# RWKV-7 scan on one core: the next level's products moved ahead of a step's outputs, state and scores on TensorE, and ScalarE reading the score banks before VectorE

## The reference, cut to what matters

```
def step(S, inp):
    r_t, w_t, k_t, v_t, kk_t, a_t = inp
    sa = einsum('bhvk,bhk->bhv', S, -kk_t)
    S = S * w_t[:, :, None, :] + sa[..., None] * (kk_t * a_t)[:, :, None, :] + v_t[..., None] * k_t[:, :, None, :]
    return S, einsum('bhvk,bhk->bhv', S, r_t)
S, y = lax.scan(step, S0, (tm(r), tm(decay), tm(k), tm(v), tm(kk), tm(a)))
```

## Time and profile before

| | us |
|---|---|
| median of 3 runs (lowest to highest) | 3029.55 (3027.71 to 3032.02) |
| the profiled execution | 3030.38 |
| its span on the core | 3028.3 |
| from the first level 0 addition of step 0 to that of step 15 (line 2957) | 918.78 to 1117.71 |

### The profile page before, as it was taken

How to read it: one execution, slowest core, us unless ns; L and a number is a source line. 1 busy time by engine, 2 the same in 40 slices (tenths; PEclk the granted TensorE clock), 3 DMA queues, 4 the chain that set the end, 5 groups by cost and what they waited for, 6 DMA issues and landing times.

```text
span 3028.3 us, 72949 instructions
## 1 busy us (share of the span) xinstructions
PE 2878.5 (95%) x29617; PEld 2731.4 (90%) x29617; DVE 1534.1 (51%) x2080; ACT 1083.7 (36%) x2139; POOL 1323.2 (44%) x959
## 2 busy tenths in 40 slices
PE   6998999998988988999999999989999999899998
PEld 6998999997978876799998899889999899799998
DVE  3435666127357775666603252476651444566612
ACT  4224333225455552433323443243332422433322
POOL 3443444442435563344443263434444344344443
PEclk8999999999999999999999999999999999899999
DMA  7544333543411004333344313433234543233332
GB/s 268 165 153 161 93 91 91 163 127 126 125 38 28 4 14 131 120 91 91 103 153 152 110 56 116 165 125 92 88 117 142 170 123 90 63 92 91 91 90 85
DMA packets 465618, 332.56 MB, mean 110 GB/s; under 512 B 19914, under 2 KB 435608, under 8 KB 465122
## 3 DMA queue, kind: packets, MB, share of 16 engines
q1 hardware_dynamic: 461400, 325.24, 34.8%
q10 hardware_dynamic: 4010, 4.22, 0.6%
HBM read 319.62 MB, written 10.20 MB: 109 GB/s over the span
## 4 chain that ended last, share of the span: by engine, by line
PE 57%; issue 4%; DVE 3%; POOL 3%; ACT 2%; DMA 0%; POOLq 0%; ACTq 0%; DVEq 0%
PE banks L1666 33%; PE banks L1674 17%; POOL ct L894 2%; PE banks L1627 1%; DVE h L2658 1%; PE banks L1689 1%; PE banks L1972 1%; DVE proj L2602 1%; PE banks L2125 0%; POOL mmt L885 0%; PE banks L1760 0%; DMA s_state<-in_state_wkv_b_dram 0%; PE banks L1695 0%; DVE proj_b L2602 0%; PE banks L2327 0%
## 5 line engine op out<-in xcount | busy, mean ns | idle before, releaser
L765 POOL TENSOR_TENSOR w_lo<-w_raw,w_hi 128x1024 fp32r<-128x1024 f32 x395 | 1005.9, 2547 | 1106.3 <-ACT w_hi L981 1086.0
L1666 PE MATMUL banks<-u_hi,w_hi 128*128 128x260 f32 x4064 | 832.7, 286 | 14.8 <-ACT w_hi L981 9.8
L1666 PE MATMUL banks<-u_lo,w_hi 128*128 128x260 f32 x4064 | 823.7, 284 | 0.0
L1666 PEld LDWEIGHTS banks<-u_hi,w_hi 128*128 128x128 f32 x4064 | 625.7, 189 | 27.6 <-issue 15.2
L1666 PEld LDWEIGHTS banks<-u_lo,w_hi 128*128 128x128 f32 x4064 | 628.4, 189 | 1.5
L981 ACT ACTIVATE w_hi<-w_raw 128x1024 fp32r<-128x1024 f32 x402 | 424.5, 1056 | 456.0 <-PE banks L1674 292.2
L1674 PE MATMUL banks<-u_hi,w_lo 128*128 128x260 f32 x4064 | 528.0, 282 | 0.0
L1674 PEld LDWEIGHTS banks<-u_hi,w_lo 128*128 128x128 f32 x4064 | 502.4, 187 | 1.6
L1666 PE MATMUL banks<-hid_hi,w_hi 128*128 128x260 f32 x1664 | 336.3, 283 | 0.0
L1666 PE MATMUL banks<-hid_lo,w_hi 128*128 128x260 f32 x1664 | 335.2, 283 | 0.0
L3107 DVE TENSOR_TENSOR csb<-proj 128x520 f32 (+1 forms) x42 | 30.6, 728 | 470.6 <-ACT proj L1048 470.6
(11 more groups left out here) (463 smaller groups left out, 3914.7 us busy)
## 6 DMA issues: line engine op xcount, KB each, us to landing
w_raw<-in_ffn_w_up_dram SPq DMA_DIRECT2D x176, 512.0 KB, 3.7
ada_raw<-in_ada_w_dram SPq DMA_DIRECT2D x96, 512.0 KB, 4.8
w_raw<-in_ffn_w_down_dram SPq DMA_DIRECT2D x64, 448.0 KB, 3.7
w_raw<-in_sconv_w_in_dram SPq DMA_DIRECT2D x48, 512.0 KB, 5.3
ada_ahead<-in_ada_w_dram SPq DMA_DIRECT2D x36, 512.0 KB, 7.3
ada_ahead_down<-in_ada_w_dram SPq DMA_DIRECT2D x36, 512.0 KB, 6.3
w_raw<-in_ffn_w_down_dram SPq DMA_DIRECT2D x32, 512.0 KB, 4.1
ada_pro<-in_ada_w_dram SPq DMA_DIRECT2D x6, 2048.0 KB, 21.5
```

What stands on the lines that cost most here:

```text
L765: pool.tensor_tensor(w_lo[:, s, :, :], w_raw[:, s, :, :], w_hi[:, s, :, :].bitcast(F32), ALU.subtract).then_inc(lo_done, 1)
L1666: pe.matmul(tile_ps[slot][half][0:width, 0:HALF], w_hi[:, s, k, 0:width], x[:, k0 + k, half * HALF:(half + 1) * HALF], start=start and k = ...
```

## The change

On TensorE a step's order becomes: update products of level 0; first products of level 1; outputs of step w - 1; first half of score part 0; update products of level 1; state products; second half of part 0; first products of level 2; right side parts 0 and 1; first half of part 1; update products of level 2; right side parts 2 and 3; second half of part 1; first products of level 3; first half of part 2; update products of level 3; second half of part 2; all of part 3; block solutions and past; values turned; passed on; inverse turned; first products of level 0 of w + 1; solutions. The values are turned in bank 7 and the inverse in bank 4, the reverse of before. ScalarE copies a score part as soon as it is made, and VectorE masks it after that. ScalarE copies the outputs of step w - 1 in step w, after its level 1 copy, and takes score part 3 before the block solution. VectorE updates the state after level 1's additions in place of level 0's, and masks a part one level later (part 3 after `receptances`). Step 0 and the last three steps are unrolled on ScalarE. The sample operations keep their places. The core of the diff:

```diff
     j, hh = n // 2, n % 2
     pair, b, rs = slice(2 * j, 2 * j + 2), bank[4 + (n + 1) % 4], slice((1 - hh) * HD, (2 - hh) * HD)
-    act.wait_ge(scores_masked, 4 * w + n + 1)
+    act.wait_ge(sc_done, 4 * w + n + 1)
...
-        ins = act.activation(uv[q][rs, :, hh, :], bank[4][rs, 0:4 * HD].rearrange("p (i t) -> p i t", i=4),
+        ins = act.activation(uv[q][rs, :, hh, :], bank[7][rs, 0:4 * HD].rearrange("p (i t) -> p i t", i=4),
...
-    act.activation(mmt[q][:, :, HD:2 * HD], bank[7][:, 4 * HD:8 * HD].rearrange("p (i t) -> p i t", i=4),
+    act.activation(mmt[q][:, :, HD:2 * HD], bank[4][:, 4 * HD:8 * HD].rearrange("p (i t) -> p i t", i=4),
...
-def scan_step(c, q, one_more, two_more):
+def outputs_out(w, c, q):
+    act.wait_ge(y_mm, 2 * w + 2)
+    act.activation(rw_y[:, 4 * q:4 * q + 4, ds(HD * c, HD)],
+                   bank[6][:, 0:4 * HD].rearrange("p (i t) -> p i t", i=4), ACT.Copy)\
+       .then_inc(y_ready, 1)
+def scan_step(c, q, one_more=True, two_more=True, first=False):
     w = 2 * c + q
     for lvl in range(1, NLV):
         first_products_out(w, lvl)
+        if lvl == 1 and not first:
+            outputs_out(w - 1, c + q - 1, 1 - q)
...
+    if one_more:
+        scores_out(w + 1, 1 - q, 3)
     block_solution_out(w)
     if one_more:
-        scores_out(w + 1, 1 - q, 3)
     solution_out(w, q)
-    act.wait_ge(y_mm, 2 * w + 2)
-    act.activation(rw_y[:, 4 * q:4 * q + 4, ds(HD * c, HD)],
-                   bank[6][:, 0:4 * HD].rearrange("p (i t) -> p i t", i=4), ACT.Copy)\
-       .then_inc(y_ready, 1)
-
...
-with act.Fori(0, NCH - 1) as c:
-    for q in range(2):
-        scan_step(c, q, True, True)
-for q in range(2):
-    scan_step(NCH - 1, q, q == 0, False)
+scan_step(0, 0, first=True)
+with act.Fori(0, NCH - 2) as c:
+    scan_step(c, 1)
+    scan_step(c + 1, 0)
+scan_step(NCH - 2, 1)
+scan_step(NCH - 1, 0, two_more=False)
+scan_step(NCH - 1, 1, one_more=False, two_more=False)
+outputs_out(2 * NCH - 1, NCH - 1, 1)
...
-        mm = both(lambda rs: bank[7][far(rs), (4 + i) * HD:(5 + i) * HD], lambda rs: mmt[q][rs, i, 0:HD],
+        mm = both(lambda rs: bank[4][far(rs), (4 + i) * HD:(5 + i) * HD], lambda rs: mmt[q][rs, i, 0:HD],
...
-        mm = both(lambda rs: bank[4][rs, i * HD:(i + 1) * HD],
+        mm = both(lambda rs: bank[7][rs, i * HD:(i + 1) * HD],
...
     update_products(w, q, 0)
+    first_products(w, q, 1)
     if w:
         outputs_of_solution(w - 1, qn)
+    if one_more:
+        scores_among(w + 1, qn, 0)
+    update_products(w, q, 1)
+    if w:
         state_products(qn)
     if one_more:
-        scores_among(w + 1, qn, 0)
         scores_of_keys(w + 1, qn, 0)
-    for lvl in range(1, NLV):
-        first_products(w, q, lvl)
-        if lvl == 1:
-            pe.wait_ge(st_updated, w + 1)
-            right_side(q, (0, 1))
-        if one_more:
-            if lvl == 1:
-                pe.wait_ge(y_ready, w + 1)
-                pe.wait_ge(srow_copied, 1)
-            elif lvl == 2:
-                pe.wait_ge(st_updated, w + 2)
-            else:
-                pe.wait_ge(rhs_ready, 2 * w + 1)
-            scores_among(w + 1, qn, lvl)
-        update_products(w, q, lvl)
-        if one_more:
-            scores_of_keys(w + 1, qn, lvl)
-        if lvl == 1:
-            right_side(q, (2, 3)).then_inc(rhs_mm, 1)
+    first_products(w, q, 2)
+    pe.wait_ge(st_updated, w + 1)
+    right_side(q, (0, 1))
+    if one_more:
+        pe.wait_ge(y_ready, w + 1)
+        pe.wait_ge(srow_copied, 1)
+        scores_among(w + 1, qn, 1)
+    update_products(w, q, 2)
+    right_side(q, (2, 3)).then_inc(rhs_mm, 1)
+    if one_more:
+        scores_of_keys(w + 1, qn, 1)
+    first_products(w, q, 3)
+    if one_more:
+        pe.wait_ge(st_updated, w + 2)
+        scores_among(w + 1, qn, 2)
+    update_products(w, q, 3)
+    if one_more:
+        scores_of_keys(w + 1, qn, 2)
+        pe.wait_ge(rhs_ready, 2 * w + 1)
+        scores_among(w + 1, qn, 3)
+        scores_of_keys(w + 1, qn, 3)
     if one_more:
         pe.wait_ge(scores_masked, 4 * w + 6)
         pe.wait_ge(tok_ready, 6 * w + 8)
     pe.wait_ge(y_ready, w + 1)
     pe.wait_ge(rhs_ready, 2 * w + 1)
     block_solutions_and_past(w, q)
+    if one_more:
+        pe.wait_ge(scores_masked, 4 * w + 7)
+        pe.wait_ge(tok_ready, 6 * w + 9)
+        turn_values(cn, qn)
     passed_on(w, q)
     if one_more:
         pe.wait_ge(scores_masked, 4 * w + 8)
         pe.wait_ge(tok_ready, 6 * w + 10)
-        turn_values(cn, qn)
         turn_inverse(w + 1, qn)
         first_products(w + 1, qn, 0)
     pe.wait_ge(rhs_ready, 2 * w + 2)
...
-    dve.wait_ge(sc_done, 4 * w + i + 1)
+    dve.wait_ge(tok_ready, 6 * w + i + 1)
...
-        if lvl == 0 and not first:
+        if lvl == 1 and not first:
             update_state(w - 1, 1 - q, one_more)
-        if one_more:
-            mask_scores(w + 1, 1 - q, lvl)
+        if one_more and lvl:
+            mask_scores(w + 1, 1 - q, lvl - 1)
...
         dve.wait_ge(y_mm, 2 * w + 1)
         receptances(c + 1, q)
+    if one_more:
+        mask_scores(w + 1, 1 - q, 3)
     dve.wait_ge(u_mm, 3 * w + 2)
```

## The result

The changed kernel takes 3054.64 us (median of 4 runs, 3052.71 to 3059.56) against 3030.14 before: 24.5 us more, ratio 1.008 with a 95% interval of 1.0066 to 1.0094. Slower was forecast, but with 9.7 us, and the range ended at 3046. The profiled execution was the slowest of the four, 3059.56.

What follows compares the result with a forecast made beforehand. The scan was taken as a chain over engines, TensorE tightest, with VectorE's sample operations holding back the level 0 additions. Each pair of steps gained 1.38 us, seven pairs 9.7, so 3029.55 became 3039 us; range 3026 to 3046.

Steps and rivals of the forecast that it cites:

- The ring: Scan step from level 0 additions to the next ones: even 13.67 us against 12.52, odd 14.75 against 14.52.
- X: Time from level 0 additions to the block solutions in a scan step: taken as 9.1 us, ends 8.4 and 9.4.
- Sign (a): VectorE's level 0 additions still start where the sample operation ends; level 0 update products start over 1.2 us before them.
- sign (b): TensorE waits over 1 us per step on line 2957 ahead of level 1 first products, and none on `uv`.
- The clock: TensorE's granted clock in the scan, read as 1.00 (2.4 GHz) before the change; no term for its falling.
- The pair of reference: Two scan steps around 1010 us before the change, 12.52 and 14.52, sum 27.04 us; forecast 28.42, seven pairs.
- The masks at 0: VectorE's masks a level later delay only the inverse's turn (part 3), covered by passed on: 0 us.
- rival 2: Tail sets the pace: level 0 update products and additions come 0.6 us earlier per step, 3021 us; chance 0.14.
- Block solution behind part 3 at 0: ScalarE copies score part 3 ahead of the block solution, two instructions of 0.53 us: cost 0, ends 0 and 0.5.
- Rival 3: ScalarE's score part 3 holds the block solution: 0.3 us per step, 4.2 us more, 3043 us; chance 0.10.
- Rival 1: TensorE's filler covers every hole of the stretch, X is 8.41, nothing changes: 3029.5 us; chance 0.20.
- The drain at a change of tile shape: TensorE between 64-row and 128-row products: 0.15 us per exit counted; an equal entry cost would add 2.1 us total.

Runs made afterwards that it cites:

- e13: The changed kernel unchanged, timed once more beside the filler on the same chip: 3051.95 us, ratio 1.0069.
- e2: Changed kernel with the sample operations spread, some moved behind the next step's level 0 additions: 3037.03 us, ratio 1.0024 to the kernel before.
- e7: e2 with values and inverse turned into the free right halves of banks 1 and 3, without the mask waits there: 3031.11 us, ratio 1.0005.
- e8: Kernel before, TensorE's old order for levels, outputs, state and scores, with the change's other parts, free bank halves and sample operations spread: 3021.01 us.
- e6: Kernel before with one part alone, the level 1 first products right behind the level 0 update products: 3046.44 us, ratio 1.0051.
- e4: Kernel before with the sample operations spread as in e2: 3031.77 us, ratio 1.0005.
- e3: Changed kernel with one part undone, the level 1 first products behind outputs and the first half of score part 0 again: 3037.57 us, ratio 1.0026.
- e5: Kernel before with one part alone, ScalarE copying score parts first and VectorE masking afterwards, a level later: 3028.55 us, ratio 0.9997.
- e11: Kernel before with the tail alone: values turned ahead of passed on, values and inverse in free halves of banks 1 and 3: 3031.73 us, ratio 1.0006.
- e9: e1 with as many identity product pairs again in the array's other two corners, on the changed kernel: 3058.27 us, ratio 1.0092.
- e1: Changed kernel with TensorE's wait filled by unread products, 15 pairs of 64 columns in even steps, 8 in odd: 3048.96 us, ratio 1.0062.
- e12: Changed kernel with TensorE's wait filled by unread products, 4 pairs of 256 columns in even steps, 2 in odd: 3045.36 us, ratio 1.0046.

## Why the prediction was right or wrong

**The ring: right in its mechanism, in its sizes partly by luck.** Forecast 13.67 and 14.75 us, measured 13.60 and 14.74 in the pair shown. The two parts of a step, as medians of steps 1 to 14 in VectorE's timelines (even / odd; line 2996 is the addition to `rhs_sb`, line 2977 before):

| us | forecast | e13 | e2 | e7 | e8 | before |
|---|---|---|---|---|---|---|
| level 0 additions to line 2996 (forecast: X + 1.91) | 11.01 / 11.01 | 11.38 / 11.37 | 11.38 / 11.39 | 11.44 / 11.39 | 10.62 / 10.76 | 9.85 / 10.59 |
| line 2996 to the next additions | 2.66 / 3.74 | 2.52 / 3.37 | 2.17 / 2.18 | 1.91 / 1.93 | 1.78 / 1.81 | 2.61 / 3.74 |

The first part is usually 0.37 us longer than forecast. In the odd step the second is 0.37 shorter, because the first two sample operations take 0.69 us each where they took 0.91 and 0.83 before; the two errors cancel. In the even step they don't: 13.60 is the short one, the usual is 13.90, and e13's usual pair is 28.64 against 28.42 forecast. The mechanism, additions held back by sample operations and all queued work behind the first products, stands by e6 (15.9 us slower alone), e2 (17.6 back) and e4 (0 in the old order). What the ring left out is that its first part is long even with the additions on time (e7 against e8). Sign (a) of the forecast is in the trace in part: the additions start where the sample operation ends, but the update products of level 0 begin 1.8 us before them in one step and 1.0 in the next, where over 1.2 was asked; sign (b) likewise, with waits of 1.8 and 0.9 us in turn and none on `uv`.

**The clock: the step that failed.** The prediction read the clock of 1.00 in the earlier trace rows as a given and forecast a wait of 1.3 to 2.1 us per step without asking what TensorE's clock does after it. The changed kernel's trace answers: half clock (1.2 GHz) in parts of six even steps, each time after a wait of 1.7 to 1.8 us, 14.4 us in that execution, an estimated 10 us in the median. No term and no rival held it; without it the time would be some 3045, inside the range, which ended at 3046. A hint was there: the windows view of the kernel before, from 905 to 920 us, has a granted clock of 0.66 with TensorE busy 9.8 of 15 us. I didn't follow it up.

**The pair of reference: mis-sized.** I took 27.04 us per pair from the stretch around 1010 us. It has the one odd step of 13.44; six pairs of seven take 26.8. With 28.64 that makes 1.85 us per pair, 13 us in place of 9.7. Step 15 lost 0.9 where I had up to 0.8 gained, and step 0's addition at line 2996 came 1.8 later (929.47 against 927.64) where I had up to 0.8 (in e13 it came 0.4 earlier). Together 14 to 16, which is what remains at full clock.

**The masks at 0: wrong.** I wrote that passed on covers them. The rows show 0.33 ahead of the values and 0.41 ahead of the inverse, because each mask now stands behind ScalarE's copy, `build_rates` and `receptances`. e7 takes these waits away and is 5.9 us faster than e2 by the medians, 0.8 by the scans of the two traces. So they are a part, of uncertain size, of why e2 stayed at 3037. That rival 2 (3021) was out of reach even with the additions on time has another part, the new order itself: e7 has neither late additions nor these waits and stands at 3031.

**Block solution behind part 3 at 0: right.** Block to passed on is 1.23 us in the trace (1.18 before). Block to its copy is 0.79 (955.98 to 956.77; 0.75 before). Rival 3 didn't happen. Rival 1 (X of 8.4) didn't either. **The drain at a change of tile shape**, for which the Trainium skill's page "TensorEngine Tiling (Array Packing)" was cited, was not tested apart. X came out at 9.03 us in the even and 9.24 in the odd step, one near each of the two figures worked out for it (9.1 and 9.25), so these runs don't tell whether the entry costs too.

What stays open: how often the clock falls in executions without a trace, what decides whether it falls after a wait of 1.8 us, and what e3's 7 us over the kernel before consist of. Its trace puts some 5 of them into the steps and has the same mask waits as e2's, but no run took them out of e3.

## What to carry to other kernels

Before moving work ahead of other work, ask when its inputs come and what stands before them in the producer's queue: work that seems to delay the chain may be hiding an engine that is late, and even one that is on time. A wait that grows on TensorE may have to be priced twice, once as time and once as the clock that can fall after it. Check each part of a sum, not only the sum: two parts here were off by 0.37 us each and cancelled. And take the reference from several periods, by the starts of one line over the whole loop, not from one pair.

## What was not expected of the hardware

The granted clock fell to half in the changed kernel's scan within 2 us after the end of single waits of 1.7 to 1.8 us, in six steps of one execution and two of another. It held in the traces of e6 and e2, with waits up to 1.4 and 0.6 us there, and it also held in most even steps of e13 with the long wait. From step 2 on no fall came without such a wait before it. That the wait makes it fall is the reading of this timing and of the filler runs, not shown by itself. Two changes that are worth nothing alone, e5 (-1.8 us, within its interval) and e11 (+0.5, likewise), are worth 13.3 us together with part 3's earlier copy: each alone only handed the wait to the other's resource. Part 3's copy never ran alone, so its share isn't known. And TensorE idled without any semaphore in the middle of its products, up to 1.3 us at a time between matmuls, where 30 pairs of small products per even step had been added (e9). With 15 (e1) there is no such hole between matmuls in the same view, with 4 wide pairs (e12) two of 0.2 us; e8, without any filler, has eight of up to 0.7 us.
